# Down projections of two MLPs by a seven-product scheme, and alternating copies in a windowed attention

## What is computed

```python
u = rmsnorm(h, norm_mlp_g) @ w_up                      # 1024 -> 4096
h = h + jnp.square(jax.nn.relu(u)) @ w_down            # 4096 -> 1024
...
h2 = rms_norm(x, ln2_g)                                # second block, same form
x = x + jnp.square(jax.nn.relu(h2 @ w_ff1)) @ w_ff2
...
scores = einsum(q_blk, kg) + bias                      # 8 heads of 64, windows of rows x columns
scores = where(valid, scores, -1e30)
out = einsum(softmax(scores), vg)
```

## Time and profile before

| | us |
|---|---|
| median of three executions | 3198.01 (3194.74 to 3199.88) |
| profiled execution, its own time | 3200.11 |
| its span in the trace | 3198.3 |
| granted TensorE clock, mean | 0.993 |
| TensorE matmul busy | 3114.6 (97%) |
| DVE busy | 1357.9 (42%) |
| POOL busy | 1051.2 (33%) |
| ACT busy | 790.8 (25%) |

### The profile page before, as it was taken

How to read it: one execution, slowest core, us unless ns; L and a number is a source line. 1 busy time by engine, 2 the same in 40 slices (tenths; PEclk the granted TensorE clock), 3 DMA queues, 4 the chain that set the end, 5 groups by cost and what they waited for, 6 DMA issues and landing times.

```text
span 3198.3 us, 39032 instructions
## 1 busy us (share of the span) xinstructions
PE 3114.6 (97%) x14982; PEld 2467.9 (77%) x14982; DVE 1357.9 (42%) x1391; ACT 790.8 (25%) x1113; POOL 1051.2 (33%) x879
## 2 busy tenths in 40 slices
PE   8999999998999999999899999999999999999997
PEld 6776677876888888888777777886578888888886
DVE  7988873344331211113556656213675311111124
ACT  3005772124220101012253434113542201011011
POOL 3333323330333333333323333333353333333350
PEclk9999999999999999999999999999999999999999
DMA  3111002130111111111312122413031111111121
GB/s 137 46 40 33 2 30 83 47 118 7 46 47 52 47 48 51 46 50 48 112 54 75 56 72 82 155 57 132 28 119 53 46 46 53 47 46 52 46 66 53
DMA packets 50074, 194.16 MB, mean 61 GB/s; under 512 B 5680, under 2 KB 6320, under 8 KB 48560
## 3 DMA queue, kind: packets, MB, share of 16 engines
q1 hardware_dynamic: 43776, 152.50, 15.1%
q10 hardware_dynamic: 6192, 40.14, 3.3%
HBM read 171.12 MB, written 21.50 MB: 60 GB/s over the span
## 4 chain that ended last, share of the span: by engine, by line
PE 87%; DVE 7%; DMA 1%; ACT 1%; issue 1%; POOL 1%; SPq 0%; ACTq 0%; DVEq 0%; POOLq 0%
PE psum L434 72%; PE psum L838 3%; DVE cacc L1313 2%; PE psum L709 2%; PE psum L531 2%; PE psum L517 2%; PE psum L546 2%; DMA raw<-weights 1%; PE psum L758 1%; PE psum L771 1%; PE psum L660 1%; PE psum L785 1%; PE psum L640 1%; DVE P L1683 1%; DVE rstd L1300 0%
## 5 line engine op out<-in xcount | busy, mean ns | idle before, releaser
L434 PE MATMUL psum<-A_hi,w_hi 128*128 128x512 f32 x2176 | 681.5, 394 | 18.6 <-DVE A_lo L1290 13.4
L434 PE MATMUL psum<-A_lo,w_hi 128*128 128x512 f32 x2176 | 672.6, 390 | 0.0
L434 PE MATMUL psum<-A_hi,w_lo 128*128 128x512 f32 x2176 | 671.8, 390 | 0.0
L359 POOL TENSOR_TENSOR small<-ident 128x1 f32<-128x1 f32 x250 | 62.9, 252 | 1817.4 <-PE psum L434 1786.1
L365 POOL TENSOR_TENSOR w_lo<-raw,w_hi 128x1024 fp32r<-128x1024 f32 x234 | 591.9, 2529 | 19.5
L434 PEld LDWEIGHTS psum<-A_hi,w_hi 128*128 128x128 f32 x2176 | 408.9, 188 | 113.9 <-issue 27.4
L434 PEld LDWEIGHTS psum<-A_lo,w_hi 128*128 128x128 f32 x2176 | 410.1, 188 | 86.0
L434 PEld LDWEIGHTS psum<-A_hi,w_lo 128*128 128x128 f32 x2176 | 409.9, 188 | 85.7
L434 PE MATMUL psum<-B_hi,w_hi 128*128 128x512 f32 x1472 | 455.4, 391 | 3.1 <-POOL w_lo L365 2.0
L434 PE MATMUL psum<-B_hi,w_lo 128*128 128x512 f32 x1472 | 454.0, 390 | 0.0
L434 PE MATMUL psum<-B_lo,w_hi 128*128 128x512 f32 x1408 | 433.5, 389 | 0.0
(11 more groups left out here) (237 smaller groups left out, 3027.6 us busy)
## 6 DMA issues: line engine op xcount, KB each, us to landing
raw<-weights SPq DMA_DIRECT2D x256, 512.0 KB, 3.5
gate_spill<-RU SPq DMA_DIRECT2D x16, 512.0 KB, 3.1
H<-x ACTq DMA_DIRECT2D x2, 2048.0 KB, 8.6
x_spill<-H ACTq DMA_DIRECT2D x1, 4096.0 KB, 11.1
R<-gate_spill ACTq DMA_DIRECT2D x8, 512.0 KB, 4.5
mixed_spill<-t ACTq DMA_DIRECT2D x8, 512.0 KB, 2.9
BE<-rel_bias ACTq DMA_DIRECT2D x8, 512.0 KB, 4.5
MIX<-mixed_spill ACTq DMA_DIRECT2D x1, 4096.0 KB, 15.2
```

Of the source, the lines that this page charges most:

```text
L434: last = pe.matmul(PJ[s][:, c:c + step], w[:, s, k, :], b[:, k, c:c + step], start=(k == 0 and i == 0), stop=(k == kblocks - 1 and i == 2))
```

## The change

**Down projections.** `GROUPS = 6` groups of four inner tiles (24 of 32) are no longer multiplied by `job`. For such a group and a pair `j` of output tiles, `fast_down` works on a 2x2 scheme: two rows of inner tiles (two tiles each) by two output tiles, and the two halves of the tokens. Seven products of 2 inner tiles x 3 parts = 6 matmuls of 128x512, 42 in all, replace 48. They go to the four banks of `PX`. The order of the units becomes: 4 ups, then per group 2 ups, 4 downs, 2 ups (the last two of the final group left out), then ups 26 to 31, then the last 8 inner tiles by `job` as before (`last`, 8 units). There are 64 units in each MLP as before; 24 of them are `fast_down`.

**What the scheme needs.** DVE and ACT make seven combinations of the squared activations, split into high and low, in `XS` (`split_group` on ACT, `combine` on DVE, once for each two inner tiles). DVE makes four sums of weights per down unit from `raw` (`weight_sums`, one buffer `WS`), and POOL splits two parts of `raw` and then `WS` (`split_pair` and what follows it). DVE adds the products to `H` in six operations (`add_pair`). `H` is held in another basis meanwhile: `rebase` does two subtractions on half of `H` at the start of each MLP, and two additions after the last group.

```diff
+            def fast_down(q, s, layer, g, j):
+                pair = 4 * GROUPS * layer + 4 * g + j
+                wait_split(pe, q, s, "late")
+                if j == 0:
+                    pe.wait_ge(S["st_lo"], 2 * GROUPS * layer + 2 * g + 2)
+                else:
+                    pe.wait_ge(free[1 - s], q + s)
+                w12, w22 = W12[layer][s], W22[layer][s]
+                sums = (w_hi[:, s], w_lo[:, s])
+                plan = ((0, w12, 0, 0, 3 * pair, "st_done"), (2, w12, 2, 1, 0, None), (3, sums, 2, 6, 0, "st_done"),
+                        (0, sums, 4, 4, 3 * pair + 1, "st_done"), (1, w22, 0, 5, 3 * pair, "st_done"),
+                        (2, sums, 6, 2, 3 * pair + 2, None), (3, sums, 0, 3, 0, "products"))
+                for bank, w, at_w, x, read, done in plan:
+                    if read:
+                        pe.wait_ge(S["st_read"], read)
+                    for i in range(2):
+                        for t, (a, b) in enumerate(((0, 0), (0, 1), (1, 0))):
+                            last = pe.matmul(PX[:, HALF * bank:HALF * bank + HALF], w[a][:, at_w + i, :], XS[layer][:, x, b, i, :],
+                                             start=(i == 0 and t == 0), stop=(i == 1 and t == 2))
+                    if done:
+                        last.then_inc(S[done], 1)
...
+                def weight_sums(g, j):
+                    at_unit = units_of[("down", g, j)]
+                    q, s = q0 + at_unit // 2, at_unit % 2
+                    dve.wait_ge(raw_in[s], 16 * q + 16)
+                    if 4 * g + j:
+                        before = units_of[("down", g, j - 1) if j else ("down", g - 1, 3)]
+                        wait_split(dve, q0 + before // 2, before % 2, "late")
+                    k = lambda a: raw[:, s, 2 * a:2 * a + 2]
+                    to = lambda a: WS[:, 2 * a:2 * a + 2, :]
+                    chain(dve.tensor_tensor(to(0), k(2), k(3), ALU.add))
+                    dve.tensor_tensor(to(2), k(0), k(2), ALU.subtract)
+                    chain(dve.tensor_tensor(to(1), to(0), k(0), ALU.subtract))
+                    tl["st_weights"](dve.tensor_tensor(to(3), k(1), to(1), ALU.subtract))
+                def add_pair(q, s, g, j):
...
+                    dve.wait_ge(S["st_done"], 4 * pair + 1)
...
+                    tl["st_read"](dve.tensor_tensor(both(0), twice, both(0), ALU.add))
+                    dve.wait_ge(S["st_done"], 4 * pair + 2)
+                    tl["st_read"](dve.tensor_tensor(both(0), banks(2), both(0), ALU.add))
+                    for n in range(2):
+                        dve.wait_ge(S["st_done"], 4 * pair + 3 + n)
+                        out = H[:, 2 * j + 1, half_of(0)]
+                        chain(dve.tensor_tensor(out, PX[:, HALF * n:HALF * n + HALF], out, ALU.add))
+                    tl["st_read"](dve.tensor_tensor(both(1), both(1), banks(0), ALU.subtract))
+                    wait_job(dve, q, s)
+                    dve.tensor_tensor(both(1), banks(2), both(1), ALU.add).then_inc(free[s], 1)
...
+                rebase(True)
+                for at_unit in range(len(FF_UNITS) - 8):
...
+                    if unit[0] == "down":
+                        g, j = unit[1:]
+                        add_pair(q, s, g, j)
+                        if j < 2:
+                            weight_sums(g, j + 2)
+                        if j == 3:
+                            if g < GROUPS - 1:
+                                combine(2 * g + 2)
...
+                    t = unit[1]
+                    evict(q, s)
+                    if t < 4 * GROUPS:
+                        if t == 1 or t % 4 == 3:
+                            dve.wait_ge(S["st_sq"], 4 * GROUPS * layer + t + 1)
+                            combine(t // 2)
...
+                    if t >= 4 and t % 4 < 2 and t <= 4 * GROUPS + 1:
+                        weight_sums(t // 4 - 1, t % 4)
```

**Second attention.** With 5 key tiles the scores of a head are made in two pieces of 320 columns, in two banks, in place of 512 and 128; the mask reads them as two runs. In DVE's step the order becomes head by head:

```diff
-                if i + 1 < PAIRS:
-                    nb_mask(i + 1, 0)
-                    nb_mask(i + 1, 1)
-                if 1 <= i <= PAIRS:
-                    nb_copy(i - 1, 0)
-                    nb_copy(i - 1, 1)
+                for h in range(2):
+                    if i + 1 < PAIRS:
+                        nb_mask(i + 1, h)
+                    if 1 <= i <= PAIRS:
+                        nb_copy(i - 1, h)
```

More of the change, by code:

```diff
@@ L71, with ff_units @@
 MASK_W = 2 * SEQ - P
+GROUPS = 6
+def ff_units():
+    units = [("up", t) for t in range(4)]
+    for g in range(GROUPS):
+        units += [("up", 4 * g + 4), ("up", 4 * g + 5)] + [("down", g, j) for j in range(4)]
+        if g < GROUPS - 1:
+            units += [("up", 4 * g + 6), ("up", 4 * g + 7)]
+    return units + [("up", t) for t in range(26, 32)] + [("last", m) for m in range(KB)]
+FF_UNITS = ff_units()
 NB_FIRST = [0, 0, 0, 1, 2, 3, 4, 4]
@@ L76 @@
 NB_ROWS = 10
+NB_HALF = 320
 PAIRS = 4 * TT
@@ L391, in _, with split_pair, split_units @@
                 split(q, 1, lo=False)
-            splits(ROUNDS["xo"], ROUNDS["qkv2"] + 6)
+            def split_pair(q, s, layer):
+                pool.wait_ge(raw_in[s], 16 * q + 16)
+                pool.wait_ge(S["products"], 2 * q + s - 1)
+                pool.tensor_tensor(small[:, 12:13], ident[:, 0:1], ident[:, 0:1], ALU.mult)
+                hi12, lo12 = W12[layer][s]
+                hi22, lo22 = W22[layer][s]
+                chain(pool.tensor_scalar(hi12[:], raw[:, s, 0:4], 1.0, 1.0, ALU.mult, ALU.mult))
+                chain(pool.tensor_scalar(hi22[:], raw[:, s, 6:8], 1.0, 1.0, ALU.mult, ALU.mult))
+                chain(pool.tensor_tensor(lo12[:], raw[:, s, 0:4], f32(hi12[:]), ALU.subtract))
+                chain(pool.tensor_tensor(lo22[:], raw[:, s, 6:8], f32(hi22[:]), ALU.subtract))
+            def split_units(name, layer, end):
+                pool.wait_ge(S["stats"], 3 + 2 * layer)
+                pairs = 0
+                for at_unit in range(2, end):
+                    unit, q, s = FF_UNITS[at_unit], ROUNDS[name] + at_unit // 2, at_unit % 2
+                    if unit[0] != "down":
+                        split(q, s)
+                        continue
+                    split_pair(q, s, layer)
+                    pairs += 1
+                    pool.wait_ge(S["st_weights"], 4 * GROUPS * layer + pairs)
+                    chain(pool.tensor_scalar(w_hi[:, s], WS[:], 1.0, 1.0, ALU.mult, ALU.mult))
+                    pool.tensor_tensor(w_lo[:, s], WS[:], f32(w_hi[:, s]), ALU.subtract).then_inc(S["w_split"], 1)
+            splits(ROUNDS["xo"], ROUNDS["ff"])
+            split(ROUNDS["ff"], 0)
+            split(ROUNDS["ff"], 1)
+            split_units("ff", 0, len(FF_UNITS))
+            splits(ROUNDS["rec_in"], ROUNDS["qkv2"] + 6)
             split(ROUNDS["att_out"], 0)
@@ L679, in mlp @@
             def mlp(name, x, u, n, layer):
                 q0 = ROUNDS[name]
[L681 to L690, removed]
+                job(q0, 0, x, ready=norm_ready(n))
@@ L692, in _ @@
+                norm_stats(n)()
+                for at_unit in range(1, len(FF_UNITS) - 8):
+                    unit, q, s = FF_UNITS[at_unit], q0 + at_unit // 2, at_unit % 2
+                    if unit[0] == "up":
+                        job(q, s, x)
+                    else:
+                        fast_down(q, s, layer, *unit[1:])
+                if layer == 0:
+                    rounds(q0 + 28, 4, u, ready=(S["u_lo"], [k + 1 for k in range(KB)]))
             mlp("ff", A, B, 2, 0)
@@ L752, in nb_scores @@
                 to = [PX[:, 0:SEQ], PX[:, 1024:2048]] if p == 0 else PJ
-                w = P * NB_TILES[t]
-                for c in range(0, w, HALF):
-                    n = min(HALF, w - c)
+                n = HALF if NB_TILES[t] == 4 else NB_HALF
+                for c in range(P * NB_TILES[t] // n):
                     for h in range(2):
-                        rows, key = slice(DH * h, DH * h + DH), P * NB_FIRST[t] + c
-                        last = pe.matmul(to[h][:, c:c + n], Q[rows, m, P * t:P * t + P], K[rows, m, key:key + n],
-                                         start=True, stop=True)
+                        rows, key = slice(DH * h, DH * h + DH), P * NB_FIRST[t] + n * c
+                        last = pe.matmul(to[h][:, HALF * c:HALF * c + n], Q[rows, m, P * t:P * t + P],
+                                         K[rows, m, key:key + n], start=True, stop=True)
                 last.then_inc(S["scores2"], 1)
@@ L1071, in mlp, with square @@
                 norm_std(n)
[L1073 to L1082, removed]
+                def square(s, done):
+                    tallies[done](act.activation(T[s][:], T[s][:], ACT.Square))
@@ L1552, in mlp @@
                 norm_std(n)
[L1554 to L1568, removed]
+                x = XS[layer]
+                sums_made = [0]
+                def evict(q, s):
+                    wait_job(dve, q, s)
```

(41 more changed lines are left out.)

86 lines of the change are left out of this document (74 added, 12 removed).

## The result

The changed kernel takes 3214.94 us (median of five, 3212.81 to 3217.88), the kernel before 3198.01 (also over five now): a ratio of 1.0054 with a 95% interval of 1.0039 to 1.0068. It is slower by about 17 us, where the forecast was 12. Its profiled execution has a span of 3213.1 us. The kernel before was measured again beside the later runs, at 3196.87 and 3197.95; single executions of it lie between 3190 and 3200. The ratios compare means, so a difference taken from ratios can be 2 or 3 us smaller than one taken from medians.

What follows compares the result with a forecast made beforehand. TensorE, busy for 97% of the span, was taken as the bound. The MLPs' terms (+28 us) and the attention (-16) gave +12 on the profiled 3200.11, so a median of 3210 us; own range 3201 to 3221, 8 in 10 3187 to 3227.

Steps and rivals of the forecast that it cites:

- Fewer matmuls, -65.3: Down units of both MLPs: 288 fewer matmuls at 0.2267 us each, no slower with their own weights, 65.3 us less.
- The handover, 36 x 1.69: Between down units: TensorE waits for DVE's last add of the unit before, 36 times 1.69 us, 60.8 us more.
- The first unit, 12 x 1.8: Each group's first down unit: product 4 waits for DVE's first add, late behind eviction and weight sums, 21.6 us more.
- the collision: Down units: POOL operations and DVE operations with two SBUF inputs exclude each other, first-unit wait 1.45 to 2.15, not 0.55.
- j = 1 and 2, 24 x 0.2: Second and third down units of a group: product 4 waits 0.2 us behind weight sums, 4.8 us more in all.
- The start, 2 x 3.1: Start of each MLP: `rebase` delays the first eviction, so TensorE's third job starts 3.1 us late, 6.2 us more.
- Queues, POOL and ACT: Down units and up jobs: POOL's splits, loads, `combine` and ACT's copies stay hidden, TensorE doesn't wait for them, no cost.
- Attention, -16: Second attention: head-by-head order starts copies earlier and shortens TensorE's stalls, step 3.75 in place of 4.49, 16 us less.
- the clock's rival: Groups: gaps lower TensorE's clock once per group, 14 us more, 3224; chance 0.15 together with both collisions at upper bounds.

Runs made afterwards that it cites:

- a2: Changed kernel, with the weight sums for the next down unit put behind the current unit's first add in DVE's queue: 3182.36 us.
- a5: Changed kernel with TensorE's wait for the last add later, weight sums behind the first add, `rebase` earlier, last add in two parts: 3112.13 us, ratio to before 0.9738.
- b1: Changed kernel, but POOL waits for the weight sums before it splits the two parts of `raw`: 3188.97 us, ratio to before 0.9981.
- c1: Kernel before with only the second attention's edits (masks and copies head by head, scores in pieces of 320): 3179.38 us, ratio 0.9951.
- c2: Kernel before with only the head-by-head order of masks and copies in the second attention: 3181.13 us, ratio 0.9946.

## Why the prediction was right

Point by point, with the MLPs measured from the sums of their first norm to their end: 876.16 to 1574.24 before and 870.51 to 1587.04 after in the first, 605.22 and 624.70 us in the second. That is 18.5 + 19.5 = 38 us more, where 28 was forecast.

- *Fewer matmuls, -65.3.* Right: 14694, and 9.52 us per unit in a2 and a5. Weights of its own for each matmul cost nothing.
- *The handover, 36 x 1.69.* Right in place and count, and in size by two small errors that cancel. The idle time is 1.59 us (the last matmul begins at 1032.05, its slot ends 0.23 later, the next begins at 1033.87): 0.26 to DVE, 1.23, and 0.10 back, where the prediction had 0.32 and 0.14. But a unit entered after a wait takes about 0.13 us more, which no term had. That makes the 1.72 of a2, and 36 x 1.72 = 61.9 in place of 60.8.
- *The first unit, 12 x 1.8.* Right in place and reason, a little small. In the group shown, its first matmul begins at 1110.06 and the next unit's at 1123.16: 13.10, against 11.11 in a2. The wait costs 1.99, 12 times: 23.9 in place of 21.6. b1 takes the collision away, and the operations fall to the 0.42 us estimated for them.
- *j = 1 and 2, 24 x 0.2.* From start to start these units take 11.49 to 11.55 in place of 11.24, so 0.25 to 0.31 each (once 0.48): 7.1 in place of 4.8.
- *The start, 2 x 3.1.* The idle time was right: the third job begins 14.36 after the second (871.66 to 886.02), 11.33 before, so 3.0. But a cost stood behind it that the term did not have: the clock fell, 1.7 + 3.0 = 4.7 us more. The prediction had put a fall of the clock into a rival, priced at one per group and held unlikely there, and never asked for it at the longest idle time of all. In the groups it did not happen.
- *Queues, POOL and ACT.* Nothing on TensorE's path, as said.
- *Attention, -16.* The second block ahead of its MLP, with the attention in it, runs from 1610.03 to 2366.89 against 1597.24 to 2370.02 before: 15.9 less. c1 has 17.5 less than the 3196.87 measured beside it, 15.7 by the ratio. The step was said to be 3.75 and is 3.74 to 3.75.

Taken together: -65.3 + 61.9 + 23.9 + 7.1 + 6.0 + 4.7 = +38, which is what the MLPs show. So every term had the right place and sign, and the MLPs' sum was 10 us too small: the clock 4.7, the first unit and j = 1 and 2 together 4.6, the handover 1.1.

That the whole came out within 5 us of the forecast is in part luck. By the terms the change costs 38 - 16 = 22 us, where 12 was forecast. The profiled execution shows only 15 more (3213.1 against 3198.3), because 5.7 us are gained ahead of the first MLP, where no edit explains it, and 1.6 elsewhere. That stretch differs between runs of the same code too: c1 reaches the first norm's sums at 872.45, c2 at 875.51, the kernel before at 876.16. What sets it stays open.

The Trainium skill states the collision as a rule ("SBUF — State Buffer", "Who interferes with whom"): a VectorE instruction with two SBUF inputs and a GpSimd instruction that reads SBUF can't run together, and the one that starts first keeps the port to its end. The traces agree: 1.40 and 0.95 us beside POOL's subtractions, 0.42 without. They are also finer than the prediction, which had the two exclude each other for their whole length. DVE's operation ends after POOL's by its own time less 0.14: 0.28 for the sums of 0.42, and 1.07 and 1.09 for the two subtractions of 1.23 in the earlier trace rows. The first sum fits too: at 1022.14 it began 0.15 before a multiplication of POOL ended and took 0.43, no longer than alone.

The Trainium skill ("TensorE: Matmul & The Clock Gate", "A second HAM failure mode: psum-queue depth-cycling") speaks for the clock's rival, from another kernel, in bf16. Here gaps of 1.4 us as drawn left the clock at 1.00, and the measurement decides.

## What to carry to other kernels

Fewer matmuls help only as far as the PSUM slots still take turns: a scheme that fills the same banks in each unit puts the last add of one unit on the path to the next, and 36 such handovers (62 us) ate nearly the whole saving of 288 matmuls (65 us). Look at each wait for what it guards (here two of four banks) and put it just ahead of that use, and look at what else stands in the queue of the engine that releases it; neither cure worked alone as it did with the other. Read the durations of short operations side by side: where one takes three times as long as its equal neighbours, look at what another engine does at that moment, and move it away to see. When a change makes TensorE wait, add up the idle times and then ask at the longest of them what the clock did after it.

## What the hardware showed that was not expected

A matmul sequence that restarts after 1.4 us of idle (as drawn) loses about 0.13 us beyond the idle time at full clock. After 2.88 us of idle, as drawn, the granted clock was 0.50 for some 3 us in one MLP and 6 in the other, which cost 1.7 and 3.0 us; with gaps of 1.4 us, three in 89 us, and one of 1.7 it stayed at 1.00. Four equal operations of 256 columns on DVE took 0.43, 1.40, 0.95 and 0.42 us beside POOL's work, and 0.41 to 0.42 each with POOL's work moved behind them.
